# The last projection of a layer and the first tile of the next, by token half, with the layer norm beside them

## The chip, the cores and the metric

One core of one Trainium2 chip runs the whole program; the other cores take no part. The metric is device time in microseconds for one launch, as the median of several runs. All times in this text are microseconds unless marked ns.

## The reference

The input is 256 tokens of width 1024 in fp32. It goes through two stacked networks of two layers each.

The **first network** (called "one" in the kernel) normalises x, multiplies it with one wide matrix, runs a sparse causal attention and a gated delta rule beside each other, mixes both by gates, and adds `mixed @ w_out` to x. After its two layers comes a final rms norm.

The **second network** ("two") is the one that the change works on. One of its layers is, cut to what matters:

```python
h = x @ w_in                                   # split into q/k/v of four branches, gates, merge rank
merged = sum(sigmoid(merge_r @ w_merge_up)[n] * ((branch[n] * silu(gate_z[n])) @ w_branch[n]) for n in range(4))
out = merged @ w_out
x = layer_norm(2**0.5 * x + out, ln_g, ln_b)   # mean and variance over the 1024 columns of a token
```

The layer norm needs all 1024 columns of a token's row, but nothing of another token's row. The next layer's `x @ w_in` needs x transposed.

## The kernel before

**Tokens and tiles.** The 256 tokens lie on 128 partitions in two halves, r = 0 and 1. A projection is cut into tiles of 512 output columns, and each tile into units of two 128-row slices of the weights. A unit is 12 matmuls of 512 columns: two slices, two token halves, three products (high by high, high by low, low by high), since fp32 values are multiplied as two parts. Both token halves of a tile lie in one PSUM tensor of 1024 columns; there are two for tiles (`bulk0`, `bulk1`, taken in turn) and two for everything else (`chain0`, `chain1`, taken in turn by `take`, line 835).

**A unit's way.** SyncE loads it into one of five `raw` slots (L716). ScalarE copies it to `w_hi`, rounded (`split`, L1200), and GpSimd subtracts to get `w_lo` (`split`, L762, the instruction is L767). `w_hi` and `w_lo` have three slots each (`SPLIT_SLOTS`, L154), so the ScalarE part of a unit waits until the matmuls of the unit three before it are done. Then TensorE runs it (`mm`, L792, the matmul is L825). A finished tile is emptied by ScalarE or VectorE, in steps called `drain_s` and `drain_v`, and a tile's first matmul waits for the drain of the tile two before it.

**Order.** All work is a list of steps in lanes, each lane in its own fixed order: "s" splits, "m" matmuls of units, "d" and "v" drains, "a" and "b" and others the small chains, "e" the layer norm. `ORDER` (L277) is a string written out by hand or by a planner that says from which lane the next step comes. Each engine runs its own part of the merged list in order, so a step that waits holds up everything behind it on that engine. The waits are on semaphores that count steps.

**End of a layer of "two".** The units of the last projection run in the order o0 k0-1, o0 k2-3, o1 k0-1, o1 k2-3, o0 k4-5, o0 k6-7, o1 k4-5, o1 k6-7. The k0-3 part of `merged` is transposed by step gT 0, the rest by gT 1; before them stand the branch tiles br11, br21, br31, br01, each with a gate tile mu, and each br tile but the first is emptied by two VectorE operations of 1024 columns (L1671 reads PSUM and SBUF, L1674 reads SBUF twice). After o1, VectorE adds the tile to x (`drain_two`, L1648, the instruction is L1658). Then `ln_a` (VectorE L2217 for half 0, ScalarE L1318 for half 1: mean, subtraction, sum of squares), `ln_s` (ScalarE L1491: a table load, then logarithm and exponential for the inverse root), `ln` (VectorE L2233: a Newton step, L1514, then L2238 and L2240 for each half with the rows `gain` and `gain2`). Only then step xT (TensorE L1038, ScalarE L1292, VectorE L2053) transposes x into `hT_hi` and `hT_lo`, and h1, the next layer's first tile, starts. Behind the last layer SyncE stores both halves with one transfer (L755).

**End of the first network's layer 0.** Step memT 0 transposes the memory input, which SyncE loads (L734) only once VectorE has done step "o 1 1" (its last operation is L1878), since it lands in that step's scratch space.

## Time and profile before

| what | value |
|---|---|
| median of 3 runs (lowest, highest) | 1166.76 (1166.55, 1167.27) |
| the profiled execution, its own time | 1166.46 |
| its span in the trace | 1164.6 |
| mean granted TensorE clock | 0.979 |
| busy: TensorE, GpSimd, VectorE, ScalarE | 1078.2, 662.5, 646.9, 584.2 |
| instructions | 16977 |

A span runs from the first to the last recorded work; the execution's own time has 1.9 around it. An engine's busy time is the sum over its instructions. Brackets behind an instruction tell how long its engine had been idle and what ended that. A granted clock of 1.00 is TensorE's upper level (2.4 GHz), 0.50 the lower (1.2 GHz).

### The profile page before, as it was taken

What the parts mean: (1) busy time and instruction counts of PE and PEld (TensorE: products, weight loads), DVE (VectorE), ACT (ScalarE), POOL (GpSimd) and SP (SyncE); (2) the same over time, 40 slices, a digit from 0 to 9 for tenths busy, and PEclk for the clock granted to TensorE, in tenths of its full rate; (3) what the DMA queues carried; (4) which work ended last, traced back from release to release, by engine and by line L of the source; (5) the groups of instructions that cost most, each with busy time, mean ns of one, the idle gap of its engine ahead of it and who ended that gap; (6) DMA issues with size and microseconds to landing.
All of it is one profiled execution on the core that took longest, in us unless ns stands there. A gap on an engine that the chain in (4) does not pass through costs nothing.

```text
span 1164.6 us, 16977 instructions
## 1 busy us (share of the span) xinstructions
PE 1078.2 (93%) x6482; PEld 943.2 (81%) x6482; DVE 646.9 (56%) x1193; ACT 584.2 (50%) x859; POOL 662.5 (57%) x288
## 2 busy tenths in 40 slices
PE   5999999999979999999999999899998949999983
PEld 4988899888868998989888887688887738887773
DVE  3765463894665446546695475426645341845543
ACT  3643336454644463336656444354685434458542
POOL 3865345763527875446675355686456728644672
PEclk9999999999989999999999999999999969999997
DMA  8544233553234655233554233554324516523340
GB/s 286 168 142 131 90 109 109 163 146 91 91 126 120 185 156 159 73 109 111 148 160 131 75 109 119 178 162 139 109 91 147 176 56 213 142 87 118 114 148 37
DMA packets 84431, 152.07 MB, mean 131 GB/s; under 512 B 10560, under 2 KB 16512, under 8 KB 84352
## 3 DMA queue, kind: packets, MB, share of 16 engines
q1 hardware_dynamic: 84352, 151.00, 43.4%
q8 instruction: 52, 0.85, 0.3%
q14 instruction: 27, 0.22, 0.1%
HBM read 149.93 MB, written 1.05 MB: 130 GB/s over the span
## 4 chain that ended last, share of the span: by engine, by line
PE 82%; DVE 8%; ACT 5%; issue 2%; POOL 1%; DMA 1%; DVEq 0%; SPq 0%; ACTq 0%; POOLq 0%
PE bulk L825 46%; PE bulk L813 12%; PE chain L902 10%; PE chain L846 5%; ACT arena L1197 2%; PE bulk L818 1%; PE chain L1161 1%; POOL w_lo L767 1%; ACT w_hi L1197 1%; PE chain L884 1%; PE chain L1011 1%; PE chain L1027 1%; DVE arena L1592 1%; PE chain L1142 1%; ACT L1196 1%
## 5 line engine op out<-in xcount | busy, mean ns | idle before, releaser
L767 POOL TENSOR_TENSOR w_lo<-raw,w_hi 128x1024 fp32r<-128x1024 f32 (+3 forms) x284 | 662.3, 2345 | 479.6 <-ACT w_hi L1197 479.1
L1197 ACT ACTIVATE w_hi<-raw 128x1024 fp32r<-128x1024 f32 (+3 forms) x284 | 285.4, 1017 | 236.7 <-PE bulk L825 205.5
L825 PE MATMUL bulk<-w_hi,hT_hi 128*128 128x512 f32 (+1 forms) x768 | 312.1, 406 | 13.0 <-DVE arena L1674 6.6
L825 PE MATMUL bulk<-w_hi,hT_lo 128*128 128x512 f32 (+1 forms) x768 | 300.3, 391 | 0.0
L825 PE MATMUL bulk<-w_lo,hT_hi 128*128 128x512 f32 (+1 forms) x768 | 300.0, 391 | 0.0
L825 PEld LDWEIGHTS bulk<-w_hi,hT_hi 128*128 128x128 f32 x768 | 145.6, 190 | 46.2 <-DVE arena L1674 8.8
L825 PEld LDWEIGHTS bulk<-w_hi,hT_lo 128*128 128x128 f32 x768 | 145.1, 189 | 30.4
L825 PEld LDWEIGHTS bulk<-w_lo,hT_hi 128*128 128x128 f32 x768 | 145.5, 189 | 27.1 <-issue 1.2
L902 PE MATMUL chain<-arena 128*128 128x128 f32 x1056 | 133.5, 277 | 7.1 <-ACT arena L1197 4.3
L902 PEld LDWEIGHTS chain<-arena 128*128 128x128 f32 x1056 | 127.0, 191 | 15.3 <-ACT arena L1197 3.5
L813 PE MATMUL bulk<-hT_hi,w_hi 128*128 128x256 f32 x384 | 110.5, 288 | 0.0
L813 PE MATMUL bulk<-hT_hi,w_lo 128*128 128x256 f32 x384 | 108.6, 283 | 0.0
L813 PE MATMUL bulk<-hT_lo,w_hi 128*128 128x256 f32 x384 | 108.6, 283 | 0.0
L1197 ACT ACTIVATE arena<-chain 128x512 f32<-128x512 f32 (+3 forms) x64 | 46.4, 746 | 111.2 <-PE chain L846 77.9
L846 PE MATMUL chain<-cst,arena 128*128 128x128 f32 (+2 forms) x512 | 72.2, 282 | 23.1 <-DVE arena L1606 11.7
L846 PEld LDWEIGHTS chain<-cst,arena 128*128 128x128 f32 (+2 forms) x512 | 61.5, 146 | 31.6 <-issue 18.2
L1196 ACT ACT_TABLE_LOAD x48 | 61.6, 1283 | 45.2 <-PE chain L1011 24.3
L813 PEld LDWEIGHTS bulk<-hT_hi,w_hi 128*128 128x128 f32 x384 | 73.7, 192 | 0.9 <-issue 0.7
L813 PEld LDWEIGHTS bulk<-hT_lo,w_hi 128*128 128x128 f32 x384 | 73.6, 192 | 0.0
L813 PEld LDWEIGHTS bulk<-hT_hi,w_lo 128*128 128x128 f32 x384 | 73.6, 192 | 0.0
L1692 DVE SCALAR_TENSOR_TENSOR arena<-bulk,par,arena 128x253 f32<-128x253 f32 (+2 forms) x144 | 59.4, 474 | 15.1 <-ACT arena L1197 13.5
L1197 ACT ACTIVATE arena<-bulk 128x1024 f32<-128x1024 f32 (+2 forms) x50 | 50.3, 1005 | 28.7 <-PE bulk L825 28.5
(231 smaller groups left out, 1302.2 us busy)
## 6 DMA issues: line engine op xcount, KB each, us to landing
raw<-in_w_in_dram SPq DMA_DIRECT2D x194, 512.0 KB, 3.6
raw<-in_w_out_dram SPq DMA_DIRECT2D x32, 512.0 KB, 4.3
raw<-in_w_branch_dram SPq DMA_DIRECT2D x16, 512.0 KB, 3.9
raw<-in_w_mem_kv_dram SPq DMA_DIRECT2D x8, 512.0 KB, 3.7
raw<-in_w_merge_up_dram SPq DMA_DIRECT2D x16, 256.0 KB, 2.8
raw<-in_w_in_dram SPq DMA_DIRECT2D x8, 420.0 KB, 3.3
gain<-in_ln_rows_dram SPq DMA_DIRECT2D x4, 512.0 KB, 5.5
gain<-in_gains_dram SPq DMA_DIRECT2D x3, 512.0 KB, 6.5
```

The costliest lines, as they stand in the source:

```text
L767: pool.tensor_tensor(lo_of(p, u)[:, 0:n], raw_of(p, u)[:, 0:n], hi_of(p, u)[:, 0:n].bitcast(F32), ALU.subtract).then_inc(p.done("split"), 1)
L813: m = pe.matmul(dst, a, b[:, kk, :], start=(kk == 0 and i == 0 and j % 2 == 0), stop=(kk == tot - 1 and i == 2 and j % 2 == 1), skip_group ...
L818: m = pe.matmul(pair[0:n, 0:S], a[:, k, :], b[:, kk, :], start=(kk == 0 and i == 0), stop=(kk == tot - 1 and i == 2))
L825: m = pe.matmul(dst, a, b[:, k, :], start=(kk == 0 and i == 0), stop=(kk == tot - 1 and i == 2))
L846: m = pe.transpose(c[0:n, i * P:i * P + v.shape[0]], v, ident[0:v.shape[0], 0:v.shape[0]])
L884: m = pe.matmul(c[:, r * 4 + j:r * 4 + j + 1], sq[:, j, r * P:(r + 1) * P], ones[:, 0:1], start=(r == 0 and j == 0), stop=(r == 1 and j == ...
L902: m = pe.matmul(c[:, j * P:(j + 1) * P], a, b, start=(j == 0), stop=(j == 3), skip_group_check=True)
L1011: m = pe.matmul(c[:, j * nk:(j + 1) * nk], qaT[:, 4 * kv + j, qb * P:(qb + 1) * P], kaT[:, kv, 0:nk], start=(j * nk % 512 == 0), stop=((j ...
L1027: m = pe.matmul(c[:, j * P:(j + 1) * P], pt[qb][:, i * P:(i + 1) * P], pq[:, k, 1280 + kv * P:1280 + (kv + 1) * P], start=(j == 0 and k == ...
L1196: act.preload_act_table_set(sets[func])
L1197: return act.activation(dst, src, func, **more)
L1692: ins = STT(cv[:, j, back:S], b[:, j * S:(j + 1) * S - back], par1[:, p.l, c:c + 1], cv[:, j, back:S], ALU.mult, ALU.add)
```

## The change

1. The last five units of the last projection (o1 k2-3, o0 k4-5, o0 k6-7, o1 k4-5, o1 k6-7) run their six matmuls for token half 0 in this order, and then their six for half 1 in the order o0 k4-5, o0 k6-7, o1 k2-3, o1 k4-5, o1 k6-7.
2. In layer 1 the four units of h1 do the same, half 1 in the order second, third, fourth, first. In layer 0 h1 stays whole.
3. Five units must now be held split at once. The first of the five lies in the free k0-3 part of `hT_hi` and `hT_lo`, the second in the k4-7 part of `sT_hi` and `sT_lo`, as does layer 1's first h1 unit; all others take the three slots in turn.
4. The o tiles are emptied by half and column block: a 512-column addition, then `bn_stats` over the 512 columns.
5. The layer norm is done by half: `bn_aggr`, one small addition, (x - mean) * gain, the inverse root and Newton step on one column, and one last operation with `gain2`. ScalarE's part of `ln_a` goes, and the sum of squares.
6. xT has four steps, one for each token half and each half of the columns, each with a chain buffer of its own.
7. The output is stored by two transfers, one for each half.
8. `ORDER` is a new string of 1160 steps in place of 1132. Of TensorE's steps in the first network, 122 of 186 in layer 0 and 124 of 183 in layer 1 keep their relative order (longest common subsequence). On TensorE gT 0 now comes after br11 in layer 0 and after br21 in layer 1, before after br31 and br21. In the first network's layer 0 the matmuls of unit g11 k6-7 now stand behind "o 1 1", before ahead of it.

```diff
+def by_half(sec, l):
+    if sec != "two":
+        return []
+    def of(*names):
+        return [n for n, x in enumerate(UNITS[sec]) if x[0] in names]
+    a, b, c, d, e = of("o0", "o1")[3:]
+    f, g, h, i = of("h1")
+    return ([[[f, g, h, i], [g, h, i, f]]] if l else []) + [[[a, b, c, d, e], [b, c, a, d, e]]]
...
-    return {"a": a, "b": b, "y": merge, "e": [("ln_a",), ("ln_s",), ("ln",)]}
+    return {"a": a, "b": b, "y": merge, "e": [(s, r) for r in range(R) for s in ("ln_a", "ln_s", "ln")]}
...
+def split_homes():
+    home, before, had = {}, {}, {}
+    ring = deque(range(SPLIT_SLOTS))
+    for x in STREAM:
+        sec, l, u = x
+        groups = [g[0] for g in by_half(sec, l)]
+        if groups and u == groups[-1][0]:
+            home[x] = IN_HT
+        elif groups and u in (groups[-1][1], groups[0][0]):
+            home[x] = IN_ST
+        else:
+            home[x] = ring[0]
+            ring.rotate(-1)
+        before[x] = had.get(home[x])
+        had[home[x]] = x
+    return home, before
...
-            sp.wait_ge(*o.after("vector", "two", DEPTH - 1, "ln"))
-            sp.dma_start(out.rearrange("a (r p) d -> p (a r) d", p=P), xs[:, :, :]).then_inc(out_sem, 16)
-            sp.wait_ge(out_sem, 16)
+            for r in range(R):
+                sp.wait_ge(*o.after("vector", "two", DEPTH - 1, "ln", r))
+                sp.dma_start(rows_out[:, r, :], xs[:, r, :]).then_inc(out_sem, 16)
+            sp.wait_ge(out_sem, 16 * R)
...
-                            for r in range(R):
+                            for r in range(R) if half is None else (half,):
...
+                def drain_o(name, b, r):
+                    c = int(name[1])
+                    xv = xs[:, r, c * 512:(c + 1) * 512]
+                    STT(xv, xv, ALPHA, b[:, r * 512:(r + 1) * 512], ALU.mult, ALU.add).then_inc(p.own, 1)
+                    v.wait_ge(*p.last())
+                    v.bn_stats(lnb[:, r, c, :], xv).then_inc(p.done("drain_v"), 1)
...
+                def ln_s(r):
+                    if r == 0:
+                        load_set(ACT.Ln)
+                    act.wait_ge(*p.after("vector", "ln_a", r))
+                    rsq(lnm[:, 2, r:r + 1], lnm[:, 3, r:r + 1]).then_inc(p.done("ln_s"), 1)
...
+                def ln_a(r):
+                    v.wait_ge(*p.after("vector", "drain_v", "o1", r))
+                    v.bn_aggr(lna[:, r, :], lnb[:, r, :, :].rearrange("p a b -> p (a b)")).then_inc(p.own, 1)
+                    v.wait_ge(*p.last())
+                    TS(lnm[:, 2, r:r + 1], lna[:, r, 1:2], LN_EPS, None, ALU.add).then_inc(p.done("ln_a"), 1)
+
+                def ln(r):
+                    u = h2[:, r, 0:D]
+                    v.wait_ge(ln_in, 32 * (p.l + 1))
+                    STT(u, xs[:, r, :], lna[:, r, 0:1], gain[:, :], ALU.subtract, ALU.mult).then_inc(p.own, 1)
+                    v.wait_ge(*p.last())
+                    v.wait_ge(*p.after("scalar", "ln_s", r))
+                    newton(lnm[:, 3, r:r + 1], lnm[:, 2, r:r + 1], lnm[:, 4, r:r + 1])
+                    STT(xs[:, r, :], u, lnm[:, 3, r:r + 1], gain2[:, :], ALU.mult, ALU.add).then_inc(p.done("ln"), 1)
+                    v.wait_ge(*p.here("ln"))
```

Around the turn from layer 0 to layer 1 the new order is, for the engines that matter:

- TensorE: o0 k0-1, o0 k2-3, gT 1, o1 k0-1, five units for half 0, five for half 1, xT 0 0, xT 0 1, h1 units 0, 1, 2 for half 0, xT 1 0, xT 1 1, unit 3 for half 0, units 1, 2, 3, 0 for half 1, then h2.
- VectorE: drain o0 half 0, drain o1 half 0, ln_a 0, ln 0, drain o0 half 1, drain o1 half 1, xT 0 0, xT 0 1, ln_a 1, ln 1, xT 1 0, xT 1 1.
- ScalarE: split of o1 k6-7, split of h1 unit 0, ln_s 0, splits of h1 units 1, 2, 3, xT 0 0, xT 0 1, ln_s 1, xT 1 0, xT 1 1. These four splits wait for the half-1 matmuls of o0 k4-5, o0 k6-7, o1 k4-5 and o1 k6-7.
- GpSimd: the same splits in the same order.

## Rows read from the trace of the kernel before

**Rows 1.** The page: busy time of TensorE, and the chain that ended last.
```profile
PE 1078.2 (93%) x6482; PEld 943.2 (81%) x6482; DVE 646.9 (56%) x1193; ACT 584.2 (50%) x859; POOL 662.5 (57%) x288
PE 82%; DVE 8%; ACT 5%; issue 2%; POOL 1%; DMA 1%; DVEq 0%; SPq 0%; ACTq 0%; POOLq 0%
```

**Rows 2.** Windows: length, busy PE, PEld, DVE, ACT, POOL, clock, DMA, GB/s.
```profile
20.00:372.00 352.00, 340.45 (x2200) 305.83 (x2199) 214.75 (x452) 167.44 (x253) 196.36 (x83) 0.99 0.44 130
...
393.00:730.00 337.00, 331.10 (x2137) 296.86 (x2136) 202.62 (x432) 172.13 (x255) 192.96 (x82) 0.99 0.43 127
```

**Rows 3.** TensorE's timeline (start, length), turn from layer 0 to 1.
```profile
935.50 0.39 PE L825 MATMUL bulk<-w_hi,hT_lo 128*128 128x512 f32 x1
949.46 3.65 PE L846 MATMUL chain<-cst,xs 128*128 128x128 f32 x16 [13.58 <-DVE xs L2240]
955.53 0.76 PE L825 MATMUL bulk<-w_hi,hT_hi 128*128 128x512 f32 x1 [2.42 <-issue]
...
967.60 0.39 PE L825 MATMUL bulk<-w_hi,hT_lo 128*128 128x512 f32 x1
967.82 0.39 PE L825 MATMUL bulk<-w_hi,hT_hi 128*128 128x512 f32 x1
```

**Rows 4.** VectorE's and ScalarE's timelines, the same turn.
```profile
944.19 1.28 DVE L2238 SCALAR_TENSOR_TENSOR xs<-xs,tiny,gain 128x1024 f32<-128x1024 f32 x1
...
941.64 1.28 ACT L1196 ACT_TABLE_LOAD   x1 [0.65 <-DVE tiny L2231]
942.93 0.44 ACT L1197 ACTIVATE tiny<-tiny 128x2 f32<-128x2 f32 x2
```

**Rows 5.** GpSimd's timeline, the same turn.
```profile
955.25 4.72 POOL L767 TENSOR_TENSOR w_lo<-raw,w_hi 128x1024 fp32r<-128x1024 f32 x2 [21.11 <-ACT w_hi L1197]
```

**Rows 6.** Groups by line: count, then busy, mean ns, then idle before.
```profile
L1197 ACT ACTIVATE w_hi<-raw 128x1024 fp32r<-128x1024 f32 (+3 forms) x284 | 285.4, 1017 | 236.7 <-PE bulk L825 205.5
...
L1671 DVE TENSOR_TENSOR arena<-arena,bulk 128x1024 f32<-128x1024 f32 x12 | 14.6, 1218 | 18.5 <-PE bulk L825 16.0 <-issue 1.9 <-DVE arena L2197 0.5
...
L2207 DVE CAST hT_hi<-chain 128x512 fp32r<-128x512 f32 x8 | 5.5, 691 | 12.4 <-PE chain L846 12.2
```

**Rows 7.** Timelines of VectorE and GpSimd where both run, in layer 1.
```profile
1005.15 0.79 DVE L1516 TENSOR_TENSOR tiny<-tiny 128x4 f32<-128x4 f32 x1 [1.10 <-ACT tiny L1197]
1005.97 1.89 DVE L1518 TENSOR_TENSOR tiny<-tiny 128x4 f32<-128x4 f32 x1
1007.89 1.92 DVE L1520 TENSOR_SCALAR tiny<-tiny 128x4 f32<-128x4 f32 x1
1009.84 0.16 DVE L1522 TENSOR_TENSOR tiny<-tiny 128x4 f32<-128x4 f32 x1
...
1003.45 6.33 POOL L767 TENSOR_TENSOR w_lo<-raw,w_hi 128x840 fp32r<-128x840 f32 x3 [1.37 <-ACT w_hi L1197]
```

**Rows 8.** Timelines of TensorE and GpSimd ahead of the last projection, layer 0.
```profile
912.39 0.47 PE L825 MATMUL bulk<-w_hi,sT_hi 128*128 128x512 f32 x1 [1.99 <-POOL w_lo L767]
...
909.88 12.77 POOL L767 TENSOR_TENSOR w_lo<-raw,w_hi 128x1024 fp32r<-128x1024 f32 x5 [4.14 <-ACT w_hi L1197]
```

**Rows 9.** Timelines at the end: the last matmul and the store.
```profile
1146.34 0.39 PE L825 MATMUL bulk<-w_hi,hT_lo 128*128 128x512 f32 x1
...
1159.83 0.39 SPq L755 DMA_DIRECT2D out_dram<-xs  x1
```

**Rows 10.** Timelines of SyncE and TensorE around memT 0, and a window there.
```profile
337.84 0.37 SPq L734 DMA_DIRECT2D arena<-in_mem_dram  x1
...
342.94 1.97 PE L846 MATMUL chain<-cst,arena 128*128 128x128 f32 x8 [4.04 <-DMA arena<-in_mem_dram]
...
340.00:345.00 5.00, 2.06 (x10) 2.07 (x11) 0.17 (x1) 4.71 (x11) 1.79 (x1) 0.55 1.03 405
```

**Rows 11.** TensorE's timeline, first tile of the second network, layer 0.
```profile
745.69 0.47 PE L825 MATMUL bulk<-w_hi,hT_hi 128*128 128x512 f32 x1 [2.75 <-DVE hT_lo L1536]
```

**Rows 12.** TensorE's timeline in the first network, a small chain's wait.
```profile
97.46 1.13 PE L902 MATMUL chain<-arena 128*128 128x128 f32 x8 [0.34 <-ACT arena L1197]
```

183 lines of the change are left out of this document (93 added, 90 removed).

## The prediction

> **What bounds the kernel now.** I read the page first, for the engine that is busy and the one that the end hangs on: both are TensorE, busy for 93% of the span and holding 82% of the chain of waits [rows 1]. So a change gains only what it takes out of TensorE's idle time (1164.6 - 1078.2 = 86.4) or out of matmuls at the lower clock. Then the timelines around the change, for where that idle time lies. At the turn of the second network's layers the last matmul of o1 ends at 935.50 + 0.39 = 935.89, the transposes start at 949.46 after 13.58 idle, h1 starts at 955.53, and h2 at 967.82 [rows 3]. From E (the end of o1) to the start of h2 it is 31.9, of which 12.6 is work: 16 transposes at 0.11 (half of 3.65/16, which ran at the lower clock) and 48 matmuls at 0.227, the step from one to the next at the upper clock [rows 3]. At the end, 1164.6 - (1146.34 + 0.39) = 17.9 follow the last matmul [rows 9]. Both stretches are what the change is about. The first network has little idle time to give: 352.0 - 340.5 = 11.6 in most of layer 0 and 337.0 - 331.1 = 5.9 in layer 1 [rows 2].
>
> **The turn, step by step.** Times are from E. The five half-0 passes are 30 matmuls at 0.227 = 6.8 and the five half-1 passes again 6.8, so half 0 of o1 is complete at -6.8 and half 0 of o0 at -9.5. VectorE adds a 512-column block in 0.69 [rows 6]. `bn_stats` stands in no row. Its bounds are 0.69 (one pass at that rate) and 1.4 (two passes); I take 0.69, as nearly every 512-column operation costs that. Both blocks of half 0 are done at -5.3, `bn_aggr` and the small addition at -4.9 (two small operations of 0.16 [rows 7]), and (x - mean) * gain takes 1.28 [rows 4], to -3.6. On ScalarE, `ln_s` 0 is queued behind the split of h1's first unit, which waits for the first half-1 pass (-5.4): split 1.0 [rows 6], table load 1.28, two functions 0.44 [rows 4], ready at -2.6. Alone, the Newton step (four of 0.16) and the last operation (1.28) would end at -0.5, before TensorE asks.
>
> But GpSimd is at work there now. In the old kernel it was idle for 21.11 during the norm [rows 5]; in the new one h1's four units are to be subtracted at -3.6, and after it as ScalarE and the half-1 passes release them, 2.4 each (4.72 for two [rows 5]), back to back until 6.4. What that does to VectorE is in [rows 7]: an operation on four columns took 0.79, 1.89 and 1.92 while GpSimd ran three subtractions in 6.33, and 0.16 once GpSimd was idle. One VectorE operation got in after each GpSimd operation. The additions out of PSUM are free of it: L1671, with one SBUF input, has a mean of 1.218 over twelve, among them ones beside GpSimd [rows 6]. The Newton step and the last operation have two SBUF inputs each, so four of them wait for four subtractions, and `ln` 0 ends at 6.5 + 1.3 = 7.9 rather than -0.5.
>
> The Trainium skill speaks against this part of the change in "SBUF — State Buffer", section Who interferes with whom: the port pair that VectorE and GpSimd share is an exclusive lock for a whole instruction, and a VectorE instruction with two SBUF inputs takes part in it. By that rule the turn comes out as here; without it, it would be the 15.0 of the first rival.
>
> Queued behind `ln` 0 on VectorE are the half-1 drains: two blocks of 0.69 + 0.69, to 10.8. Then the low part of xT 0 0 (0.69) to 11.6, and h1's first pass starts at 11.7. Three half-0 passes (1.36 each) end at 15.8. Beside them VectorE does `ln` 1, with GpSimd out of units: 12.3 for both low parts, 0.4 for the statistics, 1.28 + 0.8 + 1.28, so 16.1. Transposes 0.9, five passes 6.8: h2 starts at 23.9. The old kernel ran its transposes and its first six h1 matmuls at the lower clock after 13.58 idle [rows 3]. An idle time of 7.9 is the nearer to that one than to the 2.42 ahead of h1, so I charge the six matmuls at the lower clock again, 1.2. So 25.1 against 31.9: **-6.8**.
>
> **Ahead of the turn.** The old kernel ran five units at 2.72 each, GpSimd at 2.4 kept up. Now the five are needed within 6.8, and their subtractions take 12.0. GpSimd has a lead, since two of the five have places of their own and gT 0 comes earlier. But as these splits start earlier they meet the drains of br21, br31 and br01, whose second operation has two SBUF inputs. Working the queue through from br11 with 2.4 and 1.22 each: in layer 0 the last split ends 8.2 before E and E comes 1.7 later than in the old kernel, in layer 1 1.1 later, although the 1.99 of idle time for GpSimd [rows 8] is gone. Without collisions E would be 2.1 to 2.4 earlier. I take **+2.8** for both layers; ends -4.5 and +4.5 (a further 0.8 each for a missed slot).
>
> **The end.** Same passes, but no next splits, so GpSimd is idle. `ln` 0 is done by -1.5, the half-1 drain of o1 at 1.5, statistics 1.9, then 1.28 + 0.8 + 1.28 with gaps: 5.4. The old store went out at 1159.83 and the span ended 4.8 later [rows 9]. Half of the bytes may take a little less (0.3); bounds 0 and 1.5. 5.4 + 4.5 = 9.9 against 17.9: **-8.0**.
>
> **memT 0.** TensorE stood for 4.04 until the memory load had landed, which was issued at 337.84 when "o 1 1" was done, and ran at the lower clock after (0.55 granted in that window) [rows 10]. Twelve matmuls, 2.7, now stand between. Ends: 0, if something else holds "o 1 1" back, and -7, if all idle time goes and the matmuls of the next 5 run at twice the granted rate. I take **-4.0**: 2.7, and half of the slow time.
>
> **xT by quarter, layer 0.** TensorE waited 2.75 for the second low part ahead of h1 [rows 11]. The last step before it is now 512 columns on ScalarE and VectorE, 0.5 shorter each: **-1.0** (ends 0 and -2.5, the latter if the clock stays up). The quarters need two more chain buffers, each given back by VectorE 1.3 after its transposes, which the 0.44 of transposes doesn't hide wholly; it is in the term.
>
> **The rest of the order.** No row shows the new order. 64 and 59 of TensorE's steps in the first network moved. The two layers do the same work in different orders and differ by 11.6 - 5.9 = 5.7 in idle time [rows 2], so I take 0 with ends -5.7 and +5.7.
>
> **The sum.** -6.8 + 2.8 - 8.0 - 4.0 - 1.0 = -17.0 on the profiled execution's own 1166.5 (span 1164.6 and 1.9 around it), 0.3 below the median: about 1150.
>
> **Rivals.** *The norm isn't held up.* If VectorE's small operations slip in ahead of GpSimd's, the turn is 15.0 (first pass at 2.8, then the same passes), which gives -16.9, and E comes earlier, -4.5: -34.4, or 1132. For it: the old norm ran without a wait. Against: that was with GpSimd idle, and [rows 7]. Chance 0.18. *Half a gain.* The order of the first network takes back 5.7, memT 0 gives nothing: 1159.5. It can't be excluded, since idle time there is small and every moved step has its own waits; 0.1. *Slower.* Place: the first network's two layers, where TensorE is nearly full. Price: 0.34, what a small chain's matmuls waited for ScalarE when they came too early [rows 12]. The five terms bring 17.0, so from 50 such waits among the 123 moved steps on the kernel is slower; at 60 it gains nothing and loses 20.4, 1170. Only a careless merge does that; 0.03. *The halves don't come apart*: TensorE's queue is written out step by step, so it would take a wait on the wrong half; less than 0.01.
>
> **How the numbers follow.** My forecast has 0.69. Its own range is 1141 to 1156: the bounds of the order and of the stretch ahead of E, not all at one end. The first rival lies under it; versions in which VectorE is held up by two subtractions rather than four are near 1140. From 1132 to 1158 no more than 2 in 10 is left out: half of the first rival, the upper part of the second, and the slower one. A measurement of this kernel can tell about 0.2%, 2.3, from no change. Faster by more than that 0.95, within it 0.02, slower 0.03.
>
> **What would show it.** In the profile after: at the turn, VectorE's one-column operations of L1516 to L1522's step at 1 to 2.4 each between GpSimd's operations, `ln` 0 ending some 8 after o1's last matmul, and TensorE idle for about 8 and then 3; if they take 0.16 and TensorE idles for under 3, the first rival holds. `bn_stats` near 0.7. TensorE waiting for GpSimd ahead of the fourth and fifth half-0 pass. At the end, the last store some 5.5 behind the last matmul. memT 0's wait for the load at about 1.3. TensorE's idle time in the first network within 6 of the old. What would make me wrong: a GpSimd that is out of the way in time, or the first network slower by more than 6.

## The result, and the profile after

The changed kernel takes 1160.45 us (1159.12 to 1163.95, six runs) against 1167.01 (1166.48 to 1171.14, six runs) for the kernel before beside it: ratio 0.9941, interval 0.9922 to 0.9961. It is faster, by 6.6 where 17.0 were forecast, and the time lies above the range.

The profiled execution took 1163.95, span 1162.1, so it stands 3.5 above the median of its six; its span is 2.5 under that of before. That 3.5 matters below, where its windows are read. The page of the changed kernel, busy time of each engine:

```profile
PE 1086.8 (94%) x6482; PEld 948.4 (82%) x6482; DVE 684.2 (59%) x1213; ACT 585.9 (50%) x861; POOL 668.7 (58%) x288
```

Against [rows 1] TensorE's 6482 matmuls took 8.6 more: no matmul was added, so more of them ran at the lower clock. VectorE is busy for 37.3 more. Windows that end with the same work in both kernels show where both lie. First the kernel before (columns as in [rows 2]): the first network's layer 0 to the end of o1, its layer 1, then the second network from h1 of layer 0 to the first unit of br11, from there to E (the end of the last matmul of o1), and the turn:

```profile
0.00:371.73 371.73, 346.22 (x2223) 310.88 (x2224) 222.61 (x462) 176.18 (x264) 200.41 (x88) 0.99 0.45 137
371.73:728.62 356.89, 349.78 (x2254) 313.19 (x2253) 213.09 (x445) 181.24 (x267) 207.98 (x87) 1.00 0.44 127
745.69:896.65 150.96, 145.96 (x799) 123.63 (x799) 74.81 (x110) 87.42 (x134) 93.44 (x43) 0.99 0.47 141
896.65:935.88 39.23, 36.97 (x166) 29.49 (x166) 12.63 (x10) 15.43 (x16) 30.79 (x13) 1.00 0.59 176
935.88:967.82 31.94, 15.95 (x65) 13.36 (x65) 12.87 (x17) 12.46 (x16) 10.78 (x5) 0.68 0.23 66
```

The same five windows of the changed kernel:

```profile
0.00:378.71 378.71, 349.86 (x2223) 314.12 (x2224) 241.20 (x462) 182.18 (x269) 202.75 (x88) 0.98 0.44 134
378.71:739.17 360.46, 351.36 (x2253) 314.88 (x2253) 216.56 (x445) 185.04 (x270) 209.39 (x87) 0.99 0.43 127
756.41:909.66 153.25, 147.19 (x799) 123.53 (x799) 77.42 (x111) 87.22 (x135) 93.44 (x43) 0.98 0.46 136
909.66:949.81 40.15, 37.02 (x166) 29.49 (x166) 20.83 (x18) 19.14 (x21) 34.41 (x14) 1.00 0.57 171
949.81:974.75 24.94, 16.46 (x65) 13.32 (x65) 15.30 (x20) 6.93 (x10) 8.23 (x5) 0.73 0.38 125
```

The turn is 7.0 shorter. The first network is 7.0 and 3.6 longer, with the same number of instructions: in layer 0 VectorE's 462 take 241.20 instead of 222.61. That is where the gain went. Layer 0's 7.0 is too much for the kernel as it mostly runs, though: one_input_newton (below) has the same instructions in the same order in the first network, and its two windows there are

```profile
0.00:375.47 375.47, 348.25 (x2223) 311.83 (x2224) 240.17 (x462) 182.22 (x269) 203.54 (x88) 0.99 0.45 135
375.47:735.78 360.31, 349.68 (x2253) 313.74 (x2253) 216.63 (x445) 185.09 (x270) 209.62 (x87) 1.00 0.43 127
```

so the loss is nearer to 3.7 in layer 0 and 3.4 in layer 1: about as much in one as in the other, and 7.1 in all. The turn on VectorE and GpSimd in the changed kernel (timelines):

```profile
947.38 1.13 DVE L1595 TENSOR_TENSOR tiny<-tiny 128x1 f32<-128x1 f32 x1 [1.16 <-ACT tiny L1278]
948.54 2.30 DVE L1597 TENSOR_TENSOR tiny<-tiny 128x1 f32<-128x1 f32 x1
950.87 0.15 DVE L1599 TENSOR_SCALAR tiny<-tiny 128x1 f32<-128x1 f32 x1
951.06 2.07 DVE L1601 TENSOR_TENSOR tiny<-tiny 128x1 f32<-128x1 f32 x1
953.17 3.33 DVE L2317 SCALAR_TENSOR_TENSOR xs<-arena,tiny,gain 128x1024 f32<-128x1024 f32 x1
...
957.26 0.69 DVE L1735 BATCH_NORM_STATS2 tiny<-xs 128x6 f32<-128x512 f32 x1
...
945.66 2.82 POOL L837 TENSOR_TENSOR sT_lo<-raw,sT_hi 128x1024 fp32r<-128x1024 f32 x1 [4.37 <-ACT sT_hi L1278]
948.45 6.97 POOL L837 TENSOR_TENSOR w_lo<-raw,w_hi 128x1024 fp32r<-128x1024 f32 x3
```

`ln` 0 is held up as forecast: its Newton step and last operation end at 956.50, E + 6.7, and four subtractions hold four of its five operations. The small TENSOR_SCALAR is not one of the four. TensorE's side of it, and the last matmul:

```profile
956.65 1.94 PE L921 MATMUL chain<-cst,xs 128*128 128x128 f32 x8 [6.84 <-DVE xs L2317]
960.23 0.76 PE L900 MATMUL bulk<-sT_hi,hT_hi 128*128 128x512 f32 x1 [1.64 <-DVE tiny L1735]
...
1152.95 0.39 PE L900 MATMUL bulk<-w_hi,hT_lo 128*128 128x512 f32 x1
```

From the last matmul (1153.34) to the span's end it is 8.8, where it was 17.9 [rows 9]. Around memT 0, where 4.0 were to be won, there are three waits (0.48, 1.61 and 3.49, together 5.58) where there were two (1.43 and the 4.04 of [rows 10], together 5.47). The load goes out at 344.41, 6.6 later than in [rows 10]; in one_input_newton it goes out at 341.28, 3.4 later. Timelines of VectorE, TensorE and SyncE, and last the first of the two waits in the kernel before:

```profile
334.98 3.24 DVE L2126 TENSOR_TENSOR arena<-arena 128x1024 f32<-128x1024 f32 x1
338.25 3.30 DVE L2128 TENSOR_TENSOR arena<-arena 128x1024 f32<-128x1024 f32 x1
341.58 0.69 DVE L1958 TENSOR_TENSOR arena<-chain,tiny 128x512 f32<-128x512 f32 x1
...
341.70 1.06 PE L921 MATMUL chain<-cst,arena 128*128 128x128 f32 x8 [0.48 <-DVE arena L2128]
344.37 1.80 PE L921 MATMUL chain<-cst,arena 128*128 128x128 f32 x8 [1.61 <-DVE arena L1962]
349.67 1.97 PE L921 MATMUL chain<-cst,arena 128*128 128x128 f32 x8 [3.49 <-DMA arena<-in_mem_dram]
...
344.41 0.37 SPq L802 DMA_DIRECT2D arena<-in_mem_dram  x1
...
337.80 1.09 PE L846 MATMUL chain<-cst,arena 128*128 128x128 f32 x8 [1.43 <-DVE arena L1878]
```

L2126 and L2128 are the step mix 0. They take 1.22 each in mix0_late, where GpSimd is idle beside them; here they stand ahead of "o 1 1" (L1958 to L1962) in VectorE's queue and are held up. Another such place is the first decay tile, early in layer 0, which had no wait before. Its operations, TensorE's wait and a window in the changed kernel, and last the same wait in one_input_newton:

```profile
65.36 2.38 DVE L1833 TENSOR_SCALAR tiny<-tiny 128x8 f32<-128x8 f32 x1
67.77 2.26 DVE L1836 TENSOR_TENSOR tiny<-tiny 128x4 f32<-128x4 f32 x1
...
71.53 2.05 PE L967 MATMUL chain<-cst,tiny 128*128 128x128 f32 x8 [3.76 <-DVE tiny L1838]
...
70.00:75.00 5.00, 3.47 (x17) 3.50 (x17) 3.00 (x6) 0.00 (x0) 1.36 (x2) 0.66 0.83 254
...
71.38 1.13 PE L967 MATMUL chain<-cst,tiny 128*128 128x128 f32 x8 [1.10 <-DVE tiny L1838]
```

The 3.76 stands in this one profile. In the profiles of one_input_newton, hold_gpsimd, before_new_first, mix0_late and hold_mix, which do the same work in the same order up to there, the wait is 1.08 to 1.12. Two of the three operations are held up there and one takes 0.16, and TensorE comes later, since some of its matmuls from 62 to 70 run at the lower clock. The experiments below that aim at the 3.76 (dec_late, hold_rn) had less to win than they counted on.

### The profile page after: what moved, and what is told of

The parts are those of the page before. It is cut to its first block, busy times and chain, and to the rows that moved or that the text cites. A ratio compares the mean times of both kernels' runs of the same rounds, so it can differ in the third digit from the quotient of the medians.

```text
span 1162.1 us, 17023 instructions
## 1 busy us (share of the span) xinstructions
PE 1086.8 (94%) x6482; PEld 948.4 (82%) x6482; DVE 684.2 (59%) x1213; ACT 585.9 (50%) x861; POOL 668.7 (58%) x288
## 3 DMA queue, kind: packets, MB, share of 16 engines
HBM read 149.93 MB, written 1.05 MB: 130 GB/s over the span
## 4 chain that ended last, share of the span: by engine, by line
PE 79%; DVE 10%; ACT 5%; issue 2%; POOL 2%; DMA 1%; POOLq 0%; DVEq 0%; SPq 0%; ACTq 0%
PE bulk L900 43%; PE bulk L888 11%; PE chain L977 10%; PE chain L921 4%; ACT arena L1278 2%; PE bulk L893 2%; POOL w_lo L837 2%; PE chain L1238 1%; PE chain L959 1%; PE chain L1102 1%; ACT w_hi L1278 1%; ACT L1273 1%; PE chain L1219 1%; DVE arena L1758 1%; DVE arena L1671 1%
## 5 line engine op out<-in xcount | busy, mean ns | idle before, releaser
L837 POOL TENSOR_TENSOR w_lo<-raw,w_hi 128x1024 fp32r<-128x1024 f32 (+4 forms) x279 | 654.4, 2361 | 471.5 <-ACT w_hi L1278 471.0
L1278 ACT ACTIVATE w_hi<-raw 128x1024 fp32r<-128x1024 f32 (+4 forms) x279 | 280.1, 1016 | 250.2 <-PE bulk L900 207.8
L900 PE MATMUL bulk<-w_hi,hT_hi 128*128 128x512 f32 (+1 forms) x756 | 308.9, 409 | 13.2 <-DVE arena L1758 7.9
L900 PE MATMUL bulk<-w_hi,hT_lo 128*128 128x512 f32 (+1 forms) x756 | 296.1, 392 | 0.0
L900 PE MATMUL bulk<-w_lo,hT_hi 128*128 128x512 f32 (+1 forms) x756 | 295.6, 391 | 0.0
L921 PEld LDWEIGHTS chain<-cst,arena 128*128 128x128 f32 (+2 forms) x512 | 61.4, 146 | 30.6 <-issue 15.1
```

The costliest lines, as they stand in the source:

```text
L837: pool.tensor_tensor(lo_of(p, u)[:, 0:n], raw_of(p, u)[:, 0:n], hi_of(p, u)[:, 0:n].bitcast(F32), ALU.subtract).then_inc(p.done("split"), 1)
L900: m = pe.matmul(dst, a, b[:, k, :], start=(first and k == 0 and i == 0), stop=(last and k == nk - 1 and i == 2))
L921: m = pe.transpose(c[0:n, i * P:i * P + v.shape[0]], v, ident[0:v.shape[0], 0:v.shape[0]])
L1278: return act.activation(dst, src, func, **more)
```

## The experiments

Each version was timed beside the kernel before, whose medians were then 1167.6 to 1168.1; a ratio is against the one beside it. The changed kernel's own row was taken beside 1167.01, and none of the others was timed beside the changed kernel, so a difference from 1160.45 carries some 1 of that drift, and the ratios are the safer comparison. The changed kernel's interval is wide: those of dec_late, mix0_late, hold_gpsimd, hold_rn and hold_mix overlap it, and those of early_old and layer0_old reach just into it. Busy times are those of each page. Layer 0 is the window from 0 to the end of o1 in the first network, layer 1 the one from there to the end of its o1, in the profile of each; the profiled executions of layer0_old and hold_all were 3.9 and 2.3 above their medians, that of before_new_first 2.4 below.

| kernel | time | ratio (interval) | PE busy | DVE busy | layer 0 | layer 1 |
|---|---|---|---|---|---|---|
| changed | 1160.45 | 0.9941 (0.9922, 0.9961) | 1086.8 | 684.2 | 378.7 | 360.5 |
| first_old | 1153.08 | 0.9871 (0.9857, 0.9884) | 1080.0 | 662.1 | 371.4 | 357.0 |
| before_new_first | 1176.68 | 1.0066 (1.0053, 1.0079) | 1082.0 | 668.1 | 375.7 | 360.5 |
| bodies_old | 1153.26 | 0.9870 (0.9854, 0.9885) | 1082.0 | 661.0 | 371.7 | 357.0 |
| one_input_newton | 1153.53 | 0.9872 (0.9859, 0.9886) | 1082.9 | 677.2 | 375.5 | 360.3 |
| hold_gpsimd | 1158.17 | 0.9920 (0.9903, 0.9937) | 1085.3 | 680.6 | 375.3 | 361.3 |
| both_best | 1145.38 | 0.9804 (0.9792, 0.9817) | 1077.6 | 656.2 | 372.2 | 357.1 |
| early_old | 1157.89 | 0.9913 (0.9899, 0.9927) | 1079.0 | 681.5 | 374.3 | 358.9 |
| layer0_old | 1157.44 | 0.9912 (0.9898, 0.9927) | 1084.8 | 669.9 | 374.8 | 362.0 |
| dec_late | 1162.15 | 0.9953 (0.9940, 0.9965) | 1087.1 | 683.9 | 377.1 | 360.5 |
| mix0_late | 1164.61 | 0.9968 (0.9954, 0.9982) | 1089.1 | 677.9 | 376.0 | 362.9 |
| waits_filled | 1165.05 | 0.9973 (0.9963, 0.9984) | 1092.1 | 686.2 | 382.0 | 358.8 |
| best_filled | 1150.65 | 0.9847 (0.9831, 0.9862) | 1083.9 | 660.5 | 377.4 | 356.9 |
| hold_rn | 1160.16 | 0.9929 (0.9916, 0.9941) | 1085.4 | 678.9 | 375.7 | 360.4 |
| hold_mix | 1159.72 | 0.9928 (0.9916, 0.9940) | 1082.7 | 680.5 | 373.6 | 360.4 |
| hold_all | 1156.05 | 0.9897 (0.9883, 0.9912) | 1085.3 | 675.9 | 372.6 | 361.4 |
| best_filled_held | 1143.87 | 0.9795 (0.9782, 0.9808) | 1081.7 | 654.5 | 370.4 | 357.0 |

The two filled kernels' PE busy holds the transposes that nobody reads. hold_gpsimd, one_input_newton and before_new_first have the changed kernel's order in the whole first network, and their layer 0 is 375.3 to 375.7: the profiled execution of the changed kernel was a long one there, by about 3.2. The kernel before (371.7) and the three versions with its order there (371.4 to 372.2) show that the new order costs about 3.7 in layer 0 (the means of either group) and, by the last column, about 3.7 in layer 1.

### The order against the rest of the change

Only the string is edited (the first line of eight is shown). first_old: the steps of the first network in the old order, all else new. bodies_old: the old order in the second network too, up to the last projection. before_new_first: the kernel before with the new order in its first network.

```diff
 ORDER = (
-    "aaaaasamsvamsaasmmsassaaaaacssaccssmmcammcmmcsmasscmscmacamsmcasmssmaadcaasmaassvmamsssbmmacammsmbas"
...
+    "aaasaaammvsaasmsmasasaaaamascmcssmcammasmmcscsmsccsamcascmcmsscmaaasadsmasaamasamvmmaamsbbmssaaamsba"
...
```

> The changed kernel with the first network's steps in the order of the kernel before; the second network stays in the new order. Order theory: the missing gain went into the first network, whose end (last o1 matmul of its layer 1) is 10.6 us later in the profile after (739.2 against 728.6), 5.3 by TensorE's idle time and 6.2 by matmuls at the lower clock. So this run ends that network near 728.6 and takes 1150 to 1153 us, 8 to 10 under the changed kernel. Rival: the clock falls by chance from run to run and the order costs little; then the time stays within 2 us of 1160.5. Second rival: the ends gained less than they seem to in one profile; then it stays above 1156 although the first network ends at 728.6.

> As first_old, and in both layers of the second network the steps from h2 to br11 in the old order too; only the last projection, the turn and the end are in the new order. Order theory: the second network's layer 0 lost 2.3 us ahead of br11 (153.3 against 151.0) and layer 1 won 0.9, so this run is 1 to 2 us under first_old, near 1149.5. Rival: both orders are equal there and the 2.3 is the clock's fall behind h1's start; then it is within 1 us of first_old.

> The kernel before, with the first network's steps in the new order and nothing else of the change. Order theory: it loses what the changed kernel loses there, 8 to 11 us, so 1175 to 1178 us, with VectorE busy some 15 to 25 us longer, since its operations with two SBUF inputs meet GpSimd's subtractions at other places. Rival (the loss comes with the changed code, not with the order): 1167 us within 2.

Measured: -7.4 against the changed kernel when the old order comes back, and +8.6 against the kernel before when the new one goes in. By the ratios it is 0.0070 and 0.0066, 8.2 and 7.7. VectorE is busy for 21.2 more in before_new_first, as expected. The order of the second network's bodies is worth nothing (1153.26 against 1153.08), so bodies_old's rival holds. first_old's two windows are those of before again, with VectorE's time too:

```profile
0.00:371.40 371.40, 345.86 (x2223) 310.58 (x2224) 222.64 (x462) 176.21 (x264) 200.51 (x88) 0.99 0.45 137
371.40:728.35 356.95, 348.40 (x2254) 311.87 (x2253) 213.14 (x445) 181.12 (x267) 207.74 (x87) 1.00 0.44 127
```

So all parts of the change but this order bring 15.0 (1168.04 - 1153.08), or 16.2 by the other pair (1176.68 - 1160.45).

### The norm held up by GpSimd

one_input_newton writes the Newton step as three operations that read one column and take the others as column operands. hold_gpsimd leaves VectorE as it is and lets GpSimd wait.

```diff
-                    newton(lnm[:, 3, r:r + 1], lnm[:, 2, r:r + 1], lnm[:, 4, r:r + 1])
+                    y, x, w = lnm[:, 3, r:r + 1], lnm[:, 2, r:r + 1], lnm[:, 4, r:r + 1]
+                    TS(w, y, y, x, ALU.mult, ALU.mult).then_inc(p.own, 1)
...
+                    TS(w, w, -0.5, 1.5, ALU.mult, ALU.add).then_inc(p.own, 1)
...
+                    TS(y, y, w, None, ALU.mult).then_inc(p.own, 1)
...
```

```diff
                     pool.wait_ge(*p.after("scalar", "split", u))
+                    if (p.sec, p.l) == ("two", 1) and u < 4:
+                        pool.wait_ge(*o.after("vector", "two", 0, "ln", 0))
```

> The changed kernel with the Newton step of ln as three operations with one SBUF tensor and column operands, in place of four of which three read two SBUF tensors. Lock theory: in the turn three of the four waits of ln 0 for GpSimd go, the last operation waits for one subtraction, ln 0 ends near the end of o1's last matmul rather than 6.8 us later, and TensorE's wait ahead of xT 0 0 falls from 6.8 to under 1 us; ln 1 now meets two subtractions, so h2 starts some 18 us behind o1 rather than 24.9: 6 to 7 us less, 1154 us. Rival (a one-column operation takes part in the lock whatever its inputs, or ln 0 waits for ScalarE's inverse root): the turn stays near 25 us and the time at 1160.

> The changed kernel with one wait added: GpSimd's subtractions for the four units of layer 1's h1 wait until layer norm of token half 0 (ln 0) is done; VectorE's instructions are untouched. Theory (ln 0 takes its 8.8 us because VectorE's two-input operations alternate with GpSimd's subtractions): those operations of ln 0 fall back to some 0.1 to 0.3 us for one column and 1.3 us for the last, ln 0 ends about 5 to 6 us earlier, the subtractions start later and hold up the first units of h1 in their place for 1 to 3 us, and the turn takes 18 to 22 us in place of 24.9; time 1155 to 1159 against 1160.5. Rival (the operations on one column are slow in themselves, and the short form alone made them quick): ln 0 as long as it was, the subtractions late on top, turn 27 to 32 us, time 1163 to 1168.

VectorE in one_input_newton, then in hold_gpsimd (timelines), and GpSimd in hold_gpsimd:

```profile
944.51 0.27 DVE L2317 TENSOR_SCALAR tiny<-tiny 128x1 f32<-128x1 f32 x1 [1.16 <-ACT tiny L1278]
...
945.25 1.44 DVE L2323 SCALAR_TENSOR_TENSOR xs<-arena,tiny,gain 128x1024 f32<-128x1024 f32 x1
```

```profile
945.25 0.16 DVE L1597 TENSOR_TENSOR tiny<-tiny 128x1 f32<-128x1 f32 x1 [1.16 <-ACT tiny L1280]
...
946.02 1.28 DVE L2319 SCALAR_TENSOR_TENSOR xs<-arena,tiny,gain 128x1024 f32<-128x1024 f32 x1
...
953.29 2.22 DVE L1597 TENSOR_TENSOR tiny<-tiny 128x1 f32<-128x1 f32 x1
...
949.81 8.02 POOL L839 TENSOR_TENSOR w_lo<-raw,w_hi 128x1024 fp32r<-128x1024 f32 x3
```

With GpSimd kept away the same two-input operations on one column take 0.16 in `ln` 0, and the first two of them take 2.22 and 2.31 in `ln` 1, where the subtractions now stand. Both edits shorten the turn, from 24.9 to 17.0 and to 19.8, and the time falls by 6.9 and 2.3; the 2.3 alone is not clear of the noise, but the turn's 5.1 is read from the trace. It is the meeting with GpSimd that makes these operations slow (the lock, as the expectations call it), and not the operations themselves.

both_best has first_old's order and one_input_newton's step.

> The changed kernel with the kernel before's order in the first network, and the Newton step of layer norm as three operations that each read one column and take the other factors as column operands. Both edits alone gave 1153.1 and 1153.5 against 1160.5. Theory (the two losses are independent, since they are 580 us apart): they add, 1145 to 1147. Rival (both runs only ended the same run of pieces at half clock that one cause sets off): 1150 to 1153.

1145.38 is 15.1 under the changed kernel where the two edits alone make 7.4 + 6.9 = 14.3. They add, within what these times can tell.

### Where in the first network

early_old has the old order for the first 120 us or so, layer0_old in all of layer 0. dec_late moves one step, the first decay tile's transposes, behind two units; mix0_late moves the step mix 0 behind "o 1 1". As an example dec_late's line of the string:

```diff
-    "aaaaasamsvamsaasmmsassaaaaacssaccssmmcammcmmcsmasscmscmacamsmcasmssmaadcaasmaassvmamsssbmmacammsmbas"
+    "aaaaasamsvamsaasmmsassaaaaacssaccssmmcammcmmcsmasscmscmacamsmcsmssmaaadcaasmaassvmamsssbmmacammsmbas"
```

> The changed kernel, with the kernel before's order for the first network of layer 0 as far as the thirtieth weight unit of its projections (about the first 120 us) and the changed kernel's order after that. Theory (the loss of the new order comes in several places, and the part about the first decay tile is one of them: TensorE waits 3.76 us there and its clock is granted at half for 3.4 us after it): that wait goes and this run is 3.5 to 6 us under the changed kernel's 1160.5, at 1154.5 to 1157. Rival (it is all lost where the memory is loaded, at the end of layer 0): 1160 to 1161. Second rival (all of the loss is the early part): 1153.

> The changed kernel, with the kernel before's order in the whole of layer 0's first network, the changed kernel's order in layer 1's first network and after it. With the order of the kernel before in both layers the time was 1153.1. Theory (the loss is by layer as the stage lengths of the two profiles say, some 7 us in layer 0 and 3.6 us in layer 1, of which the times keep some two thirds): 1154.5 to 1156. Rival (layer 1's share was only the other clock of one profile): 1153.

> The changed kernel with one step moved: TensorE's transposes for the first decay tile of layer 0 stand behind the next two weight units (24 matmuls, 6 us) instead of ahead of them. Theory (those transposes wait 3.76 us for three VectorE operations on 128x4 and 128x8 that stand beside GpSimd's subtraction and take 2.38, 2.26 and 1.32 us, and nothing covers the wait): the wait goes, the same three operations stay as long as they are, and the time falls by 3 to 5.5 us to 1155 to 1157.5. Rival (what the first decay tile feeds is then late, and the wait only moves): 1160 to 1161.5, with a new wait of about 3 us at the kk step behind it.

> The changed kernel with one step moved: in layer 0's first network the two merging operations mix 0 of VectorE (3.24 and 3.30 us) stand behind its step o 1 1 instead of ahead of it. That step releases the load of the memory into the buffer, and behind it TensorE waits 3.49 us for the DMA. Theory (VectorE's queue sets when the load is issued): the load is issued some 6 us earlier, at 338 to 339 in place of 344.4, the wait for the DMA goes, the transposes of the mixed rows (mT 0) wait some 3 us more in its place, and of the 5.58 us of waits there 2 to 3.5 us are left: 1157.5 to 1159.5. Rival (the merged rows are then the last thing, so the wait only changes its name): 1160 to 1161.

The ratios fall by 0.0028 with early_old and 0.0029 with layer0_old, some 3 us each, and by a further 0.0041, 4.8 us, from layer0_old to first_old. With the windows (about 3.7 in each layer) that makes about half of the loss in each layer; the times alone cannot say which half is the larger. All four missed what was expected of them: early_old by 0.9, layer0_old by 1.4, and the two single moves altogether: neither is faster than the changed kernel, and both lie above the times of their rivals too. In dec_late the wait only moves, to the second decay tile's transposes, and is 2.21 there. In mix0_late the load goes out 6.4 earlier and TensorE no longer waits for it, but for the merged rows (timelines of SyncE and TensorE):

```profile
337.98 0.37 SPq L802 DMA_DIRECT2D arena<-in_mem_dram  x1
...
340.55 3.65 PE L921 MATMUL chain<-cst,arena 128*128 128x128 f32 x16 [3.81 <-DVE arena L2128]
```

With waits of 0.89 and 0.96 behind it that makes 5.66, as against 0.48 + 1.61 + 3.49 = 5.58 before the move. That gives nothing and costs nothing. The rise by 4 stands elsewhere: layer 0 is 376.0 long, as against 375.3 to 375.7 in the three versions with that order, and layer 1, whose order was not touched, is 362.9 as against 360.3 to 361.3, with TensorE busy for 354.2 there as against 351.4 in the changed kernel. The same matmuls take longer, so that part is the clock; why it falls more often behind this move is open.

### The clock

To tell waits from the clock that follows them, five waits of the first network got transposes of the identity that nobody reads, each into the buffer that the waiting step then writes. No wait for a semaphore is taken away; memT takes its chain buffer ahead of its wait for the load, so that the filling can stand before that wait.

```diff
-                    return chain[half_of[key]]
+                    c = chain[half_of[key]]
+                    fill(c, key)
+                    return c
+
+                def fill(c, key):
+                    for _ in range(FILL.get(key, 0)):
+                        transposes(c, [ident[:, :]] * 4)
...
```

> The changed kernel with its own order, and with transposes of the identity that nobody reads put into five waits of TensorE in the first network, each into the buffer that the waiting step then writes: 24 ahead of the first decay tile (wait 3.76 us), 24 ahead of memT 0 (3.49), 8 ahead of layer 1's first stat step (1.17), 16 ahead of its first o0 unit (2.87), 8 ahead of its pv 1 1 (1.62). Every step still waits for the same semaphore, so no wait is shorter; only the idle time is smaller. Theory (most of what the new order costs in the first network is the clock granted at half level behind these waits, about 10 us of lost speed in the changed kernel's profile against 2 to 4 with the order of before): the pieces at half level go from those five places, the two first-network stages are 4 to 8 us shorter, and the time falls to 1153 to 1157. Rival (the waits are the loss and the clock adds little): 1159.5 to 1161, the stages as long as they were.

> The version with the kernel before's order in the first network and the one-column Newton step (1145.4 us), and transposes of the identity that nobody reads in its longest data waits: 28 ahead of memT 0 (wait 3.96 us), 8 ahead of pv 1 1 and 16 ahead of mT 1 in layer 1's first network (1.44, 2.53), 8 ahead of layer 0's first xT step (1.51), 16 ahead of layer 1's first h1 unit (2.52). Its profile has two pieces at half clock, 6.83 us each, at 341 and 744 us. Theory (the clock follows TensorE's idle time): both pieces go or shrink to one of 3.4 us, and the time falls by 1.5 to 4 us to 1141.5 to 1144. Rival (the matmuls that nobody reads only delay the steps behind them, or the pieces come whatever TensorE does): 1145 to 1147.

Both missed, on the wrong side and beyond their rivals: 4.6 slower than the changed kernel and 5.3 slower than both_best, with layer 0 longer than that of the same order without filling (382.0 as against 375.3 to 375.7, 377.4 as against 372.2). The clock did what was expected of it where it was read: the granted clock from 340 to 355 is 1.00 where the changed kernel has 0.66. But the next wait grew. Windows of the changed kernel and of waits_filled, and a wait of the latter:

```profile
340.00:355.00 15.00, 9.42 (x47) 8.27 (x46) 9.89 (x12) 8.94 (x23) 6.12 (x3) 0.66 0.66 232
```

```profile
340.00:355.00 15.00, 11.98 (x83) 10.57 (x84) 10.77 (x17) 9.74 (x24) 4.70 (x3) 1.00 0.76 259
...
363.69 1.94 PE L937 MATMUL chain<-cst,arena 128*128 128x128 f32 x8 [4.61 <-DVE arena L2144]
```

What the wait hangs on is plainest in the better kernel. VectorE and GpSimd in both_best, then in best_filled:

```profile
349.56 2.19 DVE L2117 SCALAR_TENSOR_TENSOR arena<-arena,tiny 128x128 f32<-128x128 f32 x8
351.79 1.23 DVE L2126 TENSOR_TENSOR arena<-arena 128x1024 f32<-128x1024 f32 x1
...
352.57 8.39 POOL L837 TENSOR_TENSOR w_lo<-raw,w_hi 128x1024 fp32r<-128x1024 f32 x3 [6.56 <-ACT w_hi L1278]
```

```profile
348.73 4.34 DVE L2133 SCALAR_TENSOR_TENSOR arena<-arena,tiny 128x128 f32<-128x128 f32 x8
353.10 3.38 DVE L2142 TENSOR_TENSOR arena<-arena 128x1024 f32<-128x1024 f32 x1
...
350.32 5.09 POOL L846 TENSOR_TENSOR w_lo<-raw,w_hi 128x1024 fp32r<-128x1024 f32 x2 [5.03 <-ACT w_hi L1294]
```

TensorE is through with a unit sooner, ScalarE's split behind it starts at 349.11 where it was 351.37, GpSimd starts 2.25 sooner, and mix_b 1 and the first operation of mix 1 are now held up too: 4.3 more on VectorE, and a wait of 5.46 on TensorE where there was none.

### The two engines kept apart

One more wait on GpSimd at named units of layer 0, with the order left alone. hold_rn has the first entry, hold_mix the other two, hold_all all three, best_filled_held the last one on top of best_filled.

```diff
+HOLD = {
+    ('one', 0, 15): ('rn', 0),
+    ('one', 0, 73): ('mix', 0),
+    ('one', 0, 77): ('mix', 1),
+}
...
                     pool.wait_ge(*p.after("scalar", "split", u))
+                    if (p.sec, p.l, u) in HOLD:
+                        pool.wait_ge(*p.after("vector", *HOLD[(p.sec, p.l, u)]))
```

> The changed kernel with one wait added on GpSimd: its subtraction for unit 15 of layer 0's first network waits for VectorE's rn 0, the Newton step and products on 128x4 and 128x8 in front of the first decay tile. Order and all other instructions are those of the changed kernel. Theory (those three operations take 2.38, 2.26 and 1.32 us only because the subtractions for units 15, 16 and 17 stand beside them, and TensorE waits 3.76 us for them): they fall to about 0.17 us each, TensorE's wait goes to under 0.5 us, the piece at half clock behind it goes, and the time falls by 3 to 5 us to 1155.5 to 1157.5. Rival (what is gained here is lost at a later meeting of the two engines, as filling the waits showed): the wait goes and the time stays at 1159.5 to 1161.5.

> The changed kernel with two waits added on GpSimd at the end of layer 0's first network: its subtraction for unit 73 waits for VectorE's mix 0, that for unit 77 for mix 1. Theory (the load of the memory comes late, and the merged rows too, because these operations of VectorE stand beside subtractions): the two operations of mix 0 fall from 3.24 and 3.30 us to 1.23 each, the load is issued about 4 us earlier at 340.4 where it was 344.4, TensorE's units 73 and 77 come 1 to 2 us later in return, and the time falls by 2 to 4 us to 1156.5 to 1158.5. Rival (TensorE needs the weights as much as the merged rows, so the wait only changes sides): 1160 to 1162.

> The changed kernel with all three of these waits on GpSimd (unit 15 for rn 0, unit 73 for mix 0, unit 77 for mix 1). With the kernel before's order in layer 0's first network alone the time fell by 3.0 us. Theory (what the new order costs in layer 0 is these meetings of GpSimd and VectorE): at least as much comes back, 1154 to 1157.5. Rival: 1159.5 to 1162.

> The version with filled waits, old order in the first network and the one-column Newton step (1150.65 us; without the filling 1145.4), with one wait added on GpSimd: its subtraction for unit 77 of layer 0's first network waits for VectorE's mix 1. With the filling that subtraction began at 350.3 in place of 352.6 us, mix_b 1 took 4.34 us in place of 2.19 and the first operation of mix 1 3.38 in place of 1.23, and TensorE waited 5.46 us for them. Theory (the filling did what it should, and its gain was lost because a faster TensorE frees GpSimd's buffers at the moment in which VectorE merges): the 5.46 us go to under 1, the time falls by 5 to 8 us to 1142.5 to 1145.5. Rival (the transposes that nobody reads cost the time themselves): 1149 to 1151.

In hold_rn the three operations ahead of the first decay tile take 0.17, 0.16 and 0.16 and TensorE's wait of 3.76 is gone, but the time stays (1160.16): its rival holds. VectorE is busy for 4.4 less in layer 0 than in one_input_newton (235.8, 240.2) and layer 0 is as long as there (375.7, 375.5), so VectorE's held-up time is not by itself TensorE's. hold_mix brings 0.7, which can't be told from nothing and is under what was expected of it; the load goes out at 338.96 and TensorE arrives earlier too, so it still waits 3.27 for the DMA. All three holds together bring 4.4, as expected, or 0.0044 in ratio, clear of the noise. The old order in layer 0 brought 0.0029, which the intervals do not tell apart from it. In its profile layer 0 is 372.6, which is 2.9 of the 3.7 that the order costs there. best_filled_held is the clearest: one wait added, 6.8 us gained (0.0052 in ratio, 6.1). VectorE there, and GpSimd:

```profile
348.30 2.19 DVE L2140 SCALAR_TENSOR_TENSOR arena<-arena,tiny 128x128 f32<-128x128 f32 x8
350.53 1.23 DVE L2149 TENSOR_TENSOR arena<-arena 128x1024 f32<-128x1024 f32 x1
351.79 1.23 DVE L2151 TENSOR_TENSOR arena<-arena 128x1024 f32<-128x1024 f32 x1
...
353.18 11.86 POOL L853 TENSOR_TENSOR w_lo<-raw,w_hi 128x1024 fp32r<-128x1024 f32 x5 [8.37 <-DVE arena L2151]
```

No wait of over 0.8 is left to TensorE between 350 and 370. At 1143.87 it is 1.4% faster than the changed kernel and 1.9% to 2.2% faster than the kernel before. It has the lowest time of all, but both_best is not shown to be slower (0.9795 with 0.9782 to 0.9808, as against 0.9804 with 0.9792 to 0.9817). The hold without the filling, on top of both_best, was not run; both_best too has an operation of mix 1 held up (3.30 at 353.05, where the same operation takes 1.23 in best_filled_held).

## Why the prediction was wrong

The step that failed is the first network: the term for the rest of the order, put at 0, and with it memT 0, put at -4.0. Together they were to give -4.0 and measured +7.4 to +8.6. The terms for the turn and the end held.

**The turn: right, its last tenths by luck.** Forecast 31.9 to 25.1, measured 31.94 to 24.94. `bn_stats` is the 0.69 that was taken. Four subtractions held `ln` 0, as forecast; it ended 1.2 earlier because they began 0.5 earlier (945.66, E - 4.15, against -3.6) and ended at 955.42, E + 5.6, where 6.4 stood. The prediction counted the small TENSOR_SCALAR as an operation with two SBUF inputs; it has one and was not held, but the last operation waited for the fourth subtraction in its place. h1 started at E + 10.4 instead of 11.7, and TensorE lost that again: twelve matmuls came at the lower clock (5.25 from 960.23 to 965.48, where twelve steps of 0.227 are 2.7), not the six that were charged. The first rival's place was right to be named: with the Newton step out of GpSimd's way the turn is 17.0, not 15.0, and that is worth another 6.9.

**The end: right.** 17.9 to 8.8, -9.1 against -8.0. With GpSimd idle the Newton step's operations are 0.16 each, and the order of drains, statistics and norm is the one written down.

**Ahead of the turn: right in sign.** +0.9 in layer 0 and, by the same windows in layer 1, 39.2 to 39.9, +0.6; together +1.5 where +2.8 stood. Of GpSimd's subtractions there one takes 3.40, the others near 2.4 to 2.9, so about one slot was lost to the drains, by this estimate, and not more.

**xT by quarter: the size was wrong.** -1.0 stood there. From the end of o1 to h1 it is 17.07 before and 17.24 after (745.69 - 728.62 and 756.41 - 739.17). Each quarter's transposes waited for VectorE to give the chain buffer back, 1.05 and 0.71; the term named this and took it for small.

**memT 0: nothing, where -4.0 stood.** "0, if something else holds 'o 1 1' back" was named as an end and -4.0 was taken, because the matmuls that stand between were counted on TensorE's queue alone. On VectorE's queue mix 0 now runs directly ahead of "o 1 1" and beside GpSimd. The load went out later, by 6.6 in the changed kernel's profile and 3.4 in one_input_newton's, and the twelve matmuls hid only some of that: TensorE's waits there are 5.58 as against 5.47, and the clock granted from 340 to 355 is 0.66 as against 0.77. So the end at 0 is what came.

**The rest of the order: the term that cost the forecast.** It stood at 0, with ends of 5.7. The two profiles differ by 10.6 over the first network, of which the times bear out 7.4 (first_old) to 8.6 (before_new_first), memT 0 with it; the profiles of the three versions with the new order there give 7.2 to 8.0 (735.8 to 736.7 as against 728.6). Its ends were drawn from TensorE's idle time in the two layers of one kernel, and no row showed the new order. That leaves out both of the things that moved: VectorE's time grew by 18.6 + 3.5 in the two windows with not one instruction more, and TensorE's busy time by 3.6 + 1.6 through the clock. The lock that the prediction priced at the turn, where [rows 7] showed it, shows again in the first network where GpSimd subtracts beside VectorE: at mix 0 (3.24 and 3.30 for operations of 1.22) and at the first decay tile (2.38 and 2.26 for 0.17 and 0.16). The order decides where the two meet. The forecast applied it at the turn and ahead of it, and to no place in the first network.

That the order is the cause is shown both ways. That the meetings carry it is shown for layer 0, and not for all of it: three added waits on GpSimd bring 4.4 with the order untouched (hold_all), though two of the places alone bring nothing that can be told, and the clock moves from profile to profile beside it. best_filled_held shows the same mechanism with the old order. For layer 1, which has about half of the loss, nothing tells which steps it is; VectorE's time grew by only 3.5 there, and more of it may be the order of TensorE's own steps: its first o0 unit stands directly behind mT 0 and waits 2.87 for the low part of it. That wasn't tried alone.

**The sum.** In the profiles: turn -7.0, end -9.1, ahead of it +1.5, so -14.6 where -12.0 stood; first network +10.6 where -4.0 stood; xT +0.2; the second network's bodies +2.3 and -0.9. Together -2.4, the spans' 2.5 but for rounding. The median fell by 6.6 and not by 2.5 because that one profile was long, by 3.2 in layer 0 alone. The "half a gain" rival, 1159.5, had the right place and nearly the number (the order takes back 5.7, memT 0 gives nothing) and was given 0.10; it did not name the meetings of the two engines.

## What to carry to other kernels

When a hand-merged order changes, look at every engine's queue around each dependent load or long step, not at TensorE's alone, and count where GpSimd's operations meet VectorE's operations with two SBUF inputs: the sum of VectorE's busy time over the same instructions (222.6 to 241.2 here) is a quick sign of it. It is a sign and no measure: layer 1 lost as much as layer 0 with 3.5 more on VectorE. A one-column operation on a latency chain is worth writing with one SBUF input and column operands (6.9 here); on four and eight columns a TENSOR_SCALAR was held up all the same. Work that is gained in one place may move a third engine into a worse meeting, so a fix should be read at the next wait behind it; keeping the two engines apart with more waits can be worth several us (4.4 with three in hold_all, 6.8 with one in best_filled_held). And a stage should be read in more than one profile of the same code: the 3.76 wait that two experiments aimed at was 1.1 in five others.

## What the runs showed of the hardware

- A TENSOR_SCALAR on one column took 0.15 between two operations that GpSimd held up (950.87), while one on 128x8 took 2.38 (65.36) and one on 128x4 1.92 [rows 7]. The Trainium skill, "SBUF — State Buffer", section Who interferes with whom, excepts a VectorE instruction with at most one SBUF input that is outside the modes in which it uses two ports for one tensor. These rows agree, if one column can't be run in such a mode; that reading is not shown by them. Over the eighteen traces, 40 TENSOR_SCALARs on 128x1 overlap a GpSimd instruction and none took more than 0.27; of 201 on 128x4 that do, 185 took more than 0.25.
- A held-up operation costs the rest of GpSimd's current one, not a share: 1.13, 2.30, 2.07 and 3.33 for operations of 0.16, 0.16, 0.16 and 1.28, one after each subtraction. GpSimd is held up as well: three subtractions took 9.06 beside the norm in one_input_newton (from 945.57), where three took 6.97 in the changed kernel.
- The granted clock mostly fell to the lower level behind waits of TensorE of some 3 us and more (0.66 from 70 to 75 behind the 3.76), but not each time: it stayed at 1.00 behind hold_mix's 3.27, and the 2.87 of layer 1 was followed by 0.50 in the changed kernel (710 to 713) and by 1.00 in hold_rn (706.9 to 710). It also fell where no such wait stood (0.58 from 62 to 66 in hold_mix). Keeping TensorE busy in the wait kept it at 1.00 there; by itself that lost time in both kernels.
- Filling the waits lost 5.3 in both_best, and one wait on GpSimd on top of it took that back (1145.38, 1150.65, 1143.87). That the two together beat both_best is not shown.
